# Strassen block products for 17 of 22 column pairs in both up stages of an encoder layer

## The reference

```python
def swiglu_ffn(x, w_gate_up, w_down):
    g, u = jnp.split(x @ w_gate_up, 2, axis=-1)
    return (jax.nn.silu(g) * u) @ w_down
...
    r = x + 0.5 * rms_norm(swiglu_ffn(rms_norm(x, norm_ffn1_pre), w_ffn1_gate_up, w_ffn1_down), norm_ffn1_post)
    z = rms_norm(r, norm_mix_pre) @ w_in
...
    mixed = jnp.concatenate([rms_norm(attn_out, norm_attn_out), rms_norm(conv_out, norm_conv_out)], axis=-1) @ w_out
    r = r + rms_norm(mixed, norm_mix_post)
    r = r + 0.5 * rms_norm(swiglu_ffn(rms_norm(r, norm_ffn2_pre), w_ffn2_gate_up, w_ffn2_down), norm_ffn2_post)
    gate = jax.nn.sigmoid(rms_norm(r, norm_ple_pre) @ w_ple_gate)
    r = r + rms_norm(gate * (p @ w_ple_proj), norm_ple_post)
```

## Time and profile before

| | us |
|---|---|
| median of 3 runs | 1155.08 |
| lowest and highest run | 1153.62, 1156.03 |
| span of the profiled execution (first to last instruction) | 1152.4 |
| PE busy (8503 matmuls) | 1107.6 |
| DVE, ACT, POOL busy | 570.2, 422.3, 133.5 |

### The profile page before, as it was taken

One profiled execution on the slowest core, in us unless ns is written; L12 is line 12 of the kernel. 1 busy time (PEld: TensorE's weight loads), 2 busy tenths in 40 slices (PEclk: granted clock), 3 DMA queues, 4 the chain that ended last, 5 costly groups with the idle time before them and its releaser, 6 DMA issues.

```text
span 1152.4 us, 21208 instructions
## 1 busy us (share of the span) xinstructions
PE 1107.6 (96%) x8503; PEld 1076.5 (93%) x8503; DVE 570.2 (49%) x1029; ACT 422.3 (37%) x803; POOL 133.5 (12%) x154
## 2 busy tenths in 40 slices
PE   5999999999999999999989889999999999998896
PEld 5999999999999999877888889999999999998896
DVE  6644445444312268556593784445444421226743
ACT  4533333223222254423444562333323322225563
POOL 3100000000011132000213420000000001113211
PEclk8999999999999999999999999999999999999899
DMA  7232333223333205121032222233322333333002
GB/s 212 73 91 73 89 93 105 77 73 102 99 101 100 74 20 121 32 60 55 20 110 74 74 67 80 73 91 94 106 73 73 110 95 98 101 92 88 24 1 78
DMA packets 182644, 94.28 MB, mean 82 GB/s; under 512 B 11768, under 2 KB 180928, under 8 KB 182592
## 3 DMA queue, kind: packets, MB, share of 16 engines
q1 hardware_dynamic: 182576, 93.56, 28.4%
q10 hardware_dynamic: 16, 0.00, 0.0%
HBM read 91.15 MB, written 2.50 MB: 81 GB/s over the span
## 4 chain that ended last, share of the span: by engine, by line
PE 85%; DVE 10%; ACT 2%; POOL 1%; issue 1%; DMA 1%; SPq 0%; DVEq 0%; POOLq 0%; ACTq 0%
PE bank L1219 25%; PE bank L1217 25%; PE bank L1218 25%; PE bank L1247 3%; DVE x_lo L826 2%; PE misc L1326 2%; PE misc L1389 2%; DVE w_lo L796 2%; PE misc L1368 1%; POOL ssq L421 1%; DVE r L817 1%; ACT w_hi L474 1%; PE bank L1255 1%; DVE rpre L802 1%; DVE misc L802 1%
## 5 line engine op out<-in xcount | busy, mean ns | idle before, releaser
L1217 PE MATMUL bank<-x_hi,w_hi 128*128 128x272 f32 x1600 | 464.9, 291 | 5.2 <-DVE tG L1154 3.3
L1219 PE MATMUL bank<-x_hi,w_lo 128*128 128x272 f32 x1600 | 464.6, 290 | 0.0
L1218 PE MATMUL bank<-x_lo,w_hi 128*128 128x272 f32 x1600 | 461.2, 288 | 0.0
L796 DVE TENSOR_TENSOR w_lo<-raw,w_hi 128x1024 fp32r<-128x1024 f32 (+2 forms) x154 | 206.6, 1348 | 275.9 <-ACT w_hi L474 275.9
L1217 PEld LDWEIGHTS bank<-x_hi,w_hi 128*128 128x128 f32 x1600 | 302.3, 189 | 9.6 <-issue 6.7
L1218 PEld LDWEIGHTS bank<-x_lo,w_hi 128*128 128x128 f32 x1600 | 302.9, 189 | 0.1
L1219 PEld LDWEIGHTS bank<-x_hi,w_lo 128*128 128x128 f32 x1600 | 302.0, 189 | 0.0
L474 ACT ACTIVATE w_hi<-raw 128x1024 fp32r<-128x1024 f32 (+2 forms) x154 | 173.7, 1135 | 177.4 <-PE bank L1219 161.6
L1219 PE MATMUL bank<-h_hi,w_lo 128*128 128x272 f32 x704 | 204.5, 290 | 0.0
L1217 PE MATMUL bank<-h_hi,w_hi 128*128 128x272 f32 x704 | 204.2, 290 | 0.0
L1218 PE MATMUL bank<-h_lo,w_hi 128*128 128x272 f32 x704 | 203.0, 288 | 0.0
(11 more groups left out here) (160 smaller groups left out, 1073.0 us busy)
## 6 DMA issues: line engine op xcount, KB each, us to landing
raw<-w_ffn_gate_up SPq DMA_DIRECT2D x88, 512.0 KB, 3.9
raw<-w_ffn_down SPq DMA_DIRECT2D x32, 704.0 KB, 4.7
raw<-w_in SPq DMA_DIRECT2D x14, 512.0 KB, 3.9
raw<-w_ple_gate SPq DMA_DIRECT2D x8, 512.0 KB, 3.9
x_tok<-x_prompt SPq DMA_DIRECT2D x4, 512.0 KB, 5.0
raw<-w_in SPq DMA_DIRECT2D x8, 256.0 KB, 4.2
raw<-w_out SPq DMA_DIRECT2D x16, 128.0 KB, 2.9
raw<-w_out SPq DMA_DIRECT2D x8, 256.0 KB, 3.4
```

The costliest lines, as they stand in the source:

```text
L796: nc.vector.tensor_tensor(w_lo[:, s, 0:n, :], raw[:, s, 0:n, :], w_hi[:, s, 0:n, :].bitcast(F32), ALU.subtract).then_inc(lo_made, 1)
L1217: nc.tensor.matmul(psum(u), wh, hi, start=(k == 0), stop=False)
L1218: nc.tensor.matmul(psum(u), wh, lo, start=False, stop=False)
L1219: mm = nc.tensor.matmul(psum(u), wl, hi, start=False, stop=(k == n - 1))
```

## The change

In each up stage the column pairs 0 to 4 (NCL = 5) are computed as before; they make ten pairs-and-halves, which the list `PAIRS` orders. The other 17 (NJ) are "jobs". A job takes the 2 x 2 blocks (k upper or lower half, gate or up block) of a column pair and the 2 x 2 blocks of x (k half, token half A or B), and forms seven products of sums of blocks, each over 4 k tiles and 272 tokens:

- Once per stage the seven token blocks are made in `t_raw` for each of four k: DVE scales x by gain and 1/rms (`scaled_x`, L1127, four per k), POOL makes four differences and sums (`token_blocks`, L590 to L595), ACT copies the high part (`token_hi`, 1904 wide), DVE subtracts (`token_lo`, L1134).
- Once per job the weight blocks are made: DVE s31 (`first_sums`, L1147, 1024 wide), POOL s24 (`weight_sums`, L604 and L606, 512 wide), then `block_hi` on ACT and `block_lo` on DVE (L1153) in four pieces. They are made one job ahead, in two buffers (`odd_blocks`, `even_blocks`).
- The products accumulate in psum: `SEVEN` orders them as 1, 2, 3 of the job before, 6, 4 of the job before, 7, 5. ACT keeps three intermediate sums (`keep_p1`, `keep_u2`, `keep_u4`), DVE combines (`job_c11`, `job_c22`, `job_c21`) and multiplies gate and up, 544 wide (`job_hidden`).
- h stays unsplit in `h_raw`. ACT and DVE split it as the down stage begins, in seven groups of tiles (`H_GROUPS`) per half (`hidden_hi`, `hidden_lo`, L1217), and the first down product waits for it group by group. The high parts lie where the token blocks lay, so that the first copy waits for the last product.
- Buffers are laid out by hand (`at`), slots are numbered by `slot_of`, and two units of the mix stage change places. The loops over up groups are written out.

Of the two functions `jobs` in the diff the first is ACT's, the second DVE's.

```diff
+    NCL = 5
+    NJ = KF - NCL
+    PAIRS = [(i, h) for g in range(0, NCL, 2) for h in (0, 1) for i in range(g, min(g + 2, NCL))]
+    SEVEN = [(j - late, p) for j in range(NJ)
+             for p, late in ((1, 0), (2, 0), (3, 1), (6, 0), (4, 1), (7, 0), (5, 0)) if j >= late] + \
+            [(NJ - 1, 3), (NJ - 1, 4)]
+    H_GROUPS = ((0, 1), (1, 4), (4, 8), (8, 12), (12, 16), (16, 20), (20, KF))
...
+            def token_blocks(n):
+                for k in range(4):
+                    t = t_raw[:, k]
+                    pool.wait_ge(x_scaled[n], k + 1)
+                    nc.gpsimd.tensor_tensor(t[:, 3, :], t[:, 0, :], x12[:, k % 2, :], ALU.subtract).then_inc(t_made[n], 1)
...
+            def weight_sums(n, s):
+                for j in range(NJ):
+                    pool.wait_ge(s31_made[n], j + 1)
+                    if j > 1:
+                        pool.wait_ge(block_lo_made[n], 4 * (j - 1) + 3)
+                    a = job_raw(s, j)
+                    nc.gpsimd.tensor_tensor(s24(j)[:, 0, :], s31[:, 1, :], a[:, 0, :], ALU.add).then_inc(s24_made[n], 1)
+                    pool.wait_ge(s24_made[n], 2 * j + 1)
+                    nc.gpsimd.tensor_tensor(s24(j)[:, 1, :], s24(j)[:, 0, :], a[:, 1, :], ALU.add).then_inc(s24_made[n], 1)
...
+            def jobs(n, s, d):
+                for j in range(NJ):
+                    more = j + 1 < NJ
+                    if j:
+                        keep_u4(n, j - 1)
+                    if more:
+                        block_hi(n, s, j + 1, 0)
+                    keep_p1(n, j)
+                    if more:
+                        block_hi(n, s, j + 1, 1)
+                    job_gate_a(n, j)
+                    if j:
+                        job_gate_b(n, j - 1)
+                    keep_u2(n, j)
+                    if more:
+                        block_hi(n, s, j + 1, 2)
+                        block_hi(n, s, j + 1, 3)
+                    else:
+                        split_hi(C0[d]), split_hi(C0[d] + 1)
...
+            def scaled_x(n, ci, k):
+                if k > 1:
+                    dve.wait_ge(t_made[n], 4 * (k - 2) + 2)
+                t = t_raw[:, k]
+                for dst, kk, h in ((x12[:, k % 2, :], k, B), (t[:, 0, :], k, A), (t[:, 2, :], k + 4, B),
+                                   (t[:, 1, :], k + 4, A)):
+                    i = nc.vector.scalar_tensor_tensor(dst, half(r, kk, h), gain(CHAIN[ci][1], kk), rpre[:, h, :],
+                                                       ALU.mult, ALU.mult)
+                i.then_inc(x_scaled[n], 1)
...
+            def jobs(n, s, d):
+                for j in range(NJ):
+                    more = j + 1 < NJ
+                    if j:
+                        job_c22(n, j - 1)
+                    if more:
+                        first_sums(n, s, j + 1)
+                        block_lo(n, s, j + 1, 0)
+                    job_c11(n, j)
+                    if more:
+                        block_lo(n, s, j + 1, 1)
+                    if j:
+                        job_c21(n, j - 1)
+                        job_hidden(n, j - 1)
+                    if more:
+                        block_lo(n, s, j + 1, 2)
+                        block_lo(n, s, j + 1, 3)
+                    else:
+                        split_lo(C0[d]), split_lo(C0[d] + 1)
+                job_c22(n, NJ - 1)
+                job_c21(n, NJ - 1)
+                job_hidden(n, NJ - 1)
...
+            def seven(n, s):
+                for j, p in SEVEN:
+                    split, place = BLOCK[p]
+                    pe.wait_ge(block_lo_made[n], 4 * j + split + 1)
+                    if p == 1 and j < 2:
+                        pe.wait_ge(g_scaled if j == 0 else u_scaled, PAIR0[s] + 2 * NCL)
...
+                    if p == 3:
+                        pe.wait_ge(u4_kept[n], j + 1)
+                    if p == 7 and j > 1:
+                        pe.wait_ge(up_a_made[n], j - 1)
+                    if p == 4:
+                        pe.wait_ge(up_b_made[n], j + 1)
...
+                    for k in range(4):
...
+                        nc.tensor.matmul(out, hi[:, k, :], x_h, start=(k == 0 and p in (1, 2, 7)), stop=False,
+                                         skip_group_check=True)
+                        nc.tensor.matmul(out, hi[:, k, :], x_l, start=False, stop=False, skip_group_check=True)
+                        mm = nc.tensor.matmul(out, lo[:, k, :], x_h, start=False, stop=(k == 3), skip_group_check=True)
```

More of the change, by code:

```diff
@@ L310, in _, with wait_raw, load_up, load_down @@
         def _(sp):
-            def load_up(s, i):
+            def wait_raw(c):
+                b, s = before[c], stage_of[c]
+                if b is None:
+                    return
+                if s[:4] == "down" and c < C0[s] + SLOTS:
+                    sp.wait_ge(block_lo_made[FFN[s]], 4 * (NJ - 1 if c == C0[s] else NJ))
+                elif job_of(b) is not None:
+                    sp.wait_ge(block_lo_made[FFN[s]], 4 * (job_of(b) + 1))
+                else:
+                    sp.wait_ge(lo_made, split_no[b])
+            def load_up(s, first, last):
+                for c in range(C0[s] + first, C0[s] + last):
+                    j = c - C0[s]
+                    wait_raw(c)
+                    sp.dma_start(raw_up[:, slot_of[c]], up[s][j % 2, j // 2]).then_inc(w_loaded[slot_of[c]], 16)
+            def load_down(s, i):
                 for j in range(4):
@@ L911, in down_stage @@
             def down_stage(s, ci):
-                g0, last = C0[s], DOWN_GROUPS - 1
+                g0, last, n = C0[s], DOWN_GROUPS - 1, FFN[s]
+                for g in range(4):
+                    hidden_lo(n, A, g)
+                split_lo(g0 + 2)
+                for g in range(4, len(H_GROUPS)):
+                    hidden_lo(n, A, g)
+                split_lo(g0 + 3)
+                for g in range(len(H_GROUPS)):
+                    hidden_lo(n, B, g)
                 second_half(g0)
@@ L1245, in hi_pass, with lo_pass @@
                             ready()
-                        for w in (w_hi, w_lo):
-                            nc.tensor.matmul(psum(u), w[:, c % SLOTS, k, :], half(x_hi, k, h),
-                                             start=(k == 0 and w is w_hi), stop=False)
-            def lo_pass(u, c, x_lo, h, wait=None):
+                        for part in (0, 1):
+                            nc.tensor.matmul(psum(u), chunk_part(c, part)[:, k, :], high(k, h),
+                                             start=(k == 0 and part == 0), stop=False)
+            def lo_pass(u, c, low, h, wait=None):
                 for k in range(KD):
@@ L1254, in lo_pass @@
                         wait(k)
-                    mm = nc.tensor.matmul(psum(u), w_hi[:, c % SLOTS, k, :], half(x_lo, k, h),
+                    mm = nc.tensor.matmul(psum(u), chunk_part(c, 0)[:, k, :], low(k, h),
                                           start=False, stop=(k == KD - 1))
@@ L1311, in down_group @@
                         else:
                             pe.wait_ge(y_ready, i * 4 + (Y0[s] + 2 * h + m - 3))
[L1313 removed]
+                        tiles = [(c + k // MAXK, k % MAXK, half(h_hi, k, h), half(h_lo, k, h))
                                  for k in range(KF)]
                         marks = {MAXK - 1: half_used} if h == B else {}
[L1316 removed]
```

591 lines of the change are left out of this document (418 added, 173 removed).

## The result

| | before | changed |
|---|---|---|
| median time, us | 1154.35 (4 runs) | 1128.23 (4 runs, 1127.94 to 1128.60) |
| span of the profiled execution | 1152.4 | 1125.8 |
| PE busy, matmuls recorded | 1107.6, 8503 | 1064.4, 8095 |

The ratio is 0.9772, with a 95% interval of 0.9759 to 0.9784: 26.1 us faster. Forecast were 1136 us, 19 less, with 1119 to 1151 as the range.

The account below looks back on a forecast made before the run. It took the up stages to be bound by PE's number of matmuls. -51.2 (matmuls) + 19.4 (way in) + 8.0 (way out) + 4.8 (clock) = -19.0 us, from 1155.1 to 1136 us, range 1119 to 1151.

Parts of the forecast that it names:

- matmuls removed: Up stages: 84 matmuls per job in place of 96, 408 fewer in all at 0.1255 us, 51.2 us less PE work.
- way in: Before the jobs: DVE's 38.0 us of preparation makes product 1 start 9.7 us late per stage, 19.4 for both.
- middle of the stage: While jobs run: DVE, at 9.3 of 10.54 us per job, stays hidden under PE's 84 matmuls; cost 0.
- way out: Start of each down stage: PE idles while h is finished and split, 4.0 us per stage, 8.0 in all.
- clock: After four new PE stops part of the work runs at 1.2 GHz, 1.2 us each, 4.8 in all.
- my own sum: Whole kernel: the terms give 19.0 us less, 1136 us; chance 0.60 of lying within 1128 to 1144.
- a sign of being right: In the jobs: POOL's 512-wide adds would be seen with 1.3 to 2.0 us.
- it is gone when a POOL add takes over about 2.05 us: In a job's frame: the 1.2 us by which PE's matmuls cover DVE's work vanish at that length of add.
- rival (c): In the jobs: DVE and POOL bound the frame, PE stops 1.2 us in each of 34 jobs; 1176 us, chance 0.10.
- rival (a): Way in: POOL and DVE exclude each other for whole instructions, 8 us more in all; 1144 us, chance 0.14.
- DVE keeps ahead but twice: First down product: DVE's splitting of h makes PE wait 0.5 us after the first tile, 0.95 between groups 3 and 4.
- Rival (b): POOL costs DVE less: 10 us less on the way in, 4.8 less for the clock; 1121 us, chance 0.13.

Follow-up runs that it names:

- experiment 4: Changed kernel with POOL's weight sums made twice in the first up stage and three times in the second; 1223.71 us, ratio 1.0593.
- experiment 1: Changed kernel with NCL 7 in place of 5 (15 jobs, 14 classical pairs-and-halves) and reordered way-in lists; 1122.99 us, ratio 0.9723.
- experiment 5: Changed kernel with five tiles of h of half A split early, while PE runs the last products; 1124.69 us, ratio 0.9734.
- experiment 3: Changed kernel with unread matmuls filling PE's stops, 44 before the fifth pair's first half, 14 before the first down product; 1137.04 us, ratio 0.9822.
- experiment 2: Changed kernel with the token blocks' sums and differences made by DVE in place of POOL; 1131.51 us, ratio 0.9789.
- experiment 6: Changed kernel with NCL 7, the early split of five h tiles, and pairs scaled out before the next token block is split; 1112.56 us, ratio 0.9634.

## Why the prediction was right

The direction, the mechanism and the range held; the gain was 26 us, not 19. Term by term, for both stages, counted against the kernel before:

| term | forecast | measured |
|---|---|---|
| matmuls removed | -51.2 | -50.6 |
| way in, slower matmuls in it | +19.4 | +17.5 |
| middle of the stage | 0 | 0 |
| way out, PE's stops | +8.0 | +6.2 |
| clock, on the way out | +4.8 (four stops) | +3.5 |
| unchanged code | 0 | -3.2 |

The measured terms sum to -26.6, as the spans differ. The result lies at the very end of the 1128 to 1144 that I had given my own sum, and 3.2 of the 7 us that I was off come from code that the change leaves alone: no step of the forecast earns those.

**The prize.** 408 matmuls are gone. A job takes 10.58 us (POOL's first sum starts at 159.18 and 169.76 below), not 10.54. In the first up stage the 17 jobs took 180.05 us without their stop. In the kernel before, pair 4 to the first down product took 241.48 us; less 6 x 6.02 that is 205.36 for the 34 pairs and halves. So the jobs save 25.3 us, and as much in the second stage.

**The way in** was the best-sized term. I had summed 38.0 us for DVE from the scale of pair 4 to that of pair 9; it took 37.45, and product 1 started at 96.30 where I wrote 96.6. DVE on its last part, which answers to the earlier trace rows:

```profile
58.32 0.43 DVE L1105 TENSOR_TENSOR tG<-bank,rpre 128x272 f32<-128x272 f32 x1
...
81.96 2.69 DVE L1134 TENSOR_TENSOR t_lo<-t_raw,t_hi 128x1904 fp32r<-128x1904 f32 x1
84.57 2.28 DVE L1153 TENSOR_TENSOR even_blocks<-raw_up,even_blocks 128x1024 fp32r<-128x1024 f32 x1
86.77 0.43 DVE L1105 TENSOR_TENSOR tG<-bank,rpre 128x272 f32<-128x272 f32 x1
...
95.77 0.43 DVE L1105 TENSOR_TENSOR tG<-bank,rpre 128x272 f32<-128x272 f32 x1
```

Inside the sum two terms were off against each other: waiting for POOL's turns was 6.1, not 8.0, waiting for results of the others 3.8 (0.35 of it for PE), not 4.2, and DVE's own work 1.8 us more than I had counted. The lateness against PE alone is 45.06 - 36.12 = 8.9 in the first stage and 8.6 in the second, for 9.7. Its split was wrong: one long stop (5.55) and a short one (0.67), ended by job 0's last weight block and not by a gate scale, are 6.2 us; the other 2.7 us are matmuls at the lower clock.

**The frame.** "Cost of the middle of the stage 0" held. Its reasoning held only in part. A job of POOL and of DVE:

```profile
159.18 2.21 POOL L604 TENSOR_TENSOR s_rest<-s,raw_up 128x512 f32<-128x512 f32 x1 [5.79 <-DVE s L1147]
161.47 2.15 POOL L606 TENSOR_TENSOR s_rest<-s_rest,raw_up 128x512 f32<-128x512 f32 x1
169.76 2.21 POOL L604 TENSOR_TENSOR s_rest<-s,raw_up 128x512 f32<-128x512 f32 x1 [6.14 <-DVE s L1147]
```

```profile
159.02 1.22 DVE L1153 TENSOR_TENSOR odd_blocks<-raw_up,odd_blocks 128x1024 fp32r<-128x1024 f32 x1
160.16 0.43 DVE L1165 TENSOR_TENSOR tG<-misc,kept 128x272 f32<-128x272 f32 x1
160.51 1.97 DVE L1153 TENSOR_TENSOR odd_blocks<-s,odd_blocks 128x1024 fp32r<-128x1024 f32 x1
164.58 0.44 DVE L1178 TENSOR_TENSOR sq<-bank,kept 128x272 f32<-128x272 f32 x1 [2.10 <-PE bank L1721]
```

POOL's adds are seen with 2.21 and 2.15 us, above the 1.3 to 2.0 that I had given as a sign of being right. By my step "it is gone when a POOL add takes over about 2.05 us" the frame should have broken. It did not, since that step priced each add as if DVE always paid for it. Here the first add is issued at 159.18 while DVE's subtraction runs until 160.24, and ends at 161.39; DVE's next subtraction, issued at 160.51, ends at 162.48, 1.1 after that; and the second add ends 1.1 after this. They take turns by whole instructions. DVE pays once, 0.75 us (1.97 for 1.22), and stands idle 2.1 us later on. About half of each 2.2 us is POOL's waiting, as I argued against rival (c); alone the add is 1.27 (experiment 4). With that and another 0.5 of idle time at the frame's end, DVE was occupied for 8.0 us of 10.58, not 9.3.

The Trainium skill (SBUF — State Buffer, two separate sides) calls this an exclusive lock for the whole instruction, and these rows agree. My rival (a) took that to mean a higher price, 1144 us. The rule was right and the price wrong: what it costs is how long the other one must wait when it comes, which is nothing where it has nothing to do.

**The way out.** "PE's last product waits 0.65 for c22, behind two 1408-wide splits" gave the right size and the wrong cause: PE waited 0.58 for ACT's copy of product 5 (`keep_u4`, the row at 273.95 above). The stop before the first tile was 1.83 for 1.9. "DVE keeps ahead but twice", 0.5 and 0.95, was too much here: 0.21 once. The second stop exists, but the lower clock hides it. In experiment 1, whose down stage starts with the same lists and runs at full clock, it stands where I had put it:

```profile
282.38 0.39 PE L1634 MATMUL bank<-h_hi,w_split 128*128 128x272 f32 x1 [0.64 <-DVE h_lo L1225]
```

From start to start the changed kernel's three stops are 0.74, 1.99 and 0.37 us longer than the usual 0.13, 3.1 a stage. Experiment 5 took the two at the down stage away, all but some short ones, with the chain that I had named, c21, product and first split.

**The clock** is the term that was placed wrong: "The new stops ... will bring some of that ... I take 1.2 each". The clock did fall after the stops, by more than I took (0.74 on average from 87.3 to 96.3). But on the way in PE was waiting for DVE anyway, so slower matmuls only filled what would have been a longer stop (experiment 3). I had counted the lateness twice, once as DVE's and once as the clock's; that made 2.4 too many. On the way out the lower clock did stretch the sum: the down stage takes 120.2 and 120.4 us to its last group's first sum, 118.2 before. 0.4 of each is the stop. The rest, 1.6 and 1.8, is some 15 matmuls that start 0.23 us after one another in place of 0.125: they run at the 1.2 GHz level, and the mean from 277.24 to 283.20 is 0.71. Yet a full clock would have won back little of these 3.5 us, since DVE then bounds: in experiment 1 the same stretch runs at full clock and takes 119.8 us in both stages, with the second stop in it.

**Rival (b)**, 1121 us, was on the right side of both terms: it had DVE's waits smaller and the clock free, but its 10 us on the way in were 2, and on the way out the clock was not free against the kernel before. It lies 7 us below the result, my sum 8 above it.

## What to carry to other kernels

An algorithm with fewer matmuls pays as long as someone else's preparation hides under the matmuls left; the price lay in the one place where the preparation for all jobs fell due at once. There two more column pairs in the old form, as cover, paid for their extra matmuls (5.2 us less), and 14 pairs and halves as cover with an order by due times made PE's way in gapless. The better order with only ten as cover was not run, nor a kernel with less preparation, so how much of it is the cover's is open. In this kernel a lower clock cost little where DVE set the end of the stretch; before filling a stop to keep the clock up, look at who does.

## What was unexpected of the hardware

**The same code takes up to 4.4 us more or less, with the clock.** The mix and out stage was changed in none of these kernels. From the end of the first down stage to pair 4 of the next up stage it took, by the busy time by stretch (length, PE busy, ..., granted clock), in the changed kernel, in that of experiment 4, and in that of experiment 5:

```profile
412.42:672.44 260.02, 245.46 (x1740) 219.20 (x1739) 178.30 (x408) 113.27 (x288) 51.62 (x61) 0.99 0.23 63
```

```profile
435.59:694.27 258.68, 244.16 (x1739) 217.61 (x1739) 177.99 (x408) 113.31 (x288) 51.86 (x61) 0.99 0.24 63
```

```profile
409.37:672.46 263.09, 247.66 (x1740) 221.68 (x1739) 178.55 (x408) 113.29 (x288) 51.62 (x61) 0.97 0.24 62
```

DVE and ACT do the same work to 1 us; PE's busy time grows where the clock falls. Up to a stop of PE's of 2.74 us, 166 us into the stage, they run alike; the 20 us from 160 us on have the clock at 1.00 in the changed kernel and at 0.91 in experiment 5. Experiments 2 and 3 had 263.1, experiments 1 and 6 had 261.1. The end of the program moved likewise, 105.5 us in the changed kernel and 109.2 before. 3.2 of the changed kernel's 26 us lie in code that it doesn't touch, and experiment 5's profiled execution lost 4.4 of its 6.3 there.

That the change earlier in the program causes these shifts is not shown. Executions of one and the same kernel differ by as much: 1129.57 to 1137.48 in experiment 3, with mean clocks of 0.986 and 0.980, and 1122.03 to 1125.73 in experiment 5. Each kernel has one trace, so its stages are those of one execution. What decides where the clock falls was not tried. Effects under some 4 us are better read from the stage than from the median.

**Filling stops made it slower, in three of four runs.** The clock stayed up where the stops were filled, but in the profiled execution a stretch at a lower clock moved from under DVE's work into the jobs, for 4.0 us; most of the rest of the 8.8 lies in unchanged code.
